# Gated DeltaNet chunk inverses: 32x32 diagonal blocks on VectorE and two doubling levels on TensorE, in place of 16x16 blocks and three levels

## The reference

```
A = where(strict, einsum('bhncd,bhnmd->bhncm', kb, k) * decay, 0)
T = triangular_solve(A + eye, eye, left_side=True, lower=True, unit_diagonal=True)
u = T @ vb
w = T @ (kb * exp(gc)[..., None])
# then per chunk: v_new = u_c - w_c @ S;  o_c = (q_c e^gc) @ S + attn_c @ v_new
#                 S = S e^g_last + (k_c e^(g_last-gc))^T v_new
```

## Time and profile before

| | us |
|---|---|
| Median of 3 runs | 2618.58 (2617.45 to 2620.59) |
| Profiled execution | 2620.2, span 2618.4 |
| TensorE busy | 2346.7 |
| VectorE busy | 1070.3 |
| ScalarE busy | 646.9 |

### The profile page before, as it was taken

How to read it: one execution, slowest core, us unless ns; L and a number is a source line. 1 busy time by engine, 2 the same in 40 slices (tenths; PEclk the granted TensorE clock), 3 DMA queues, 4 the chain that set the end, 5 groups by cost and what they waited for, 6 DMA issues and landing times. The chain is left out here.

```text
span 2618.4 us, 35138 instructions
## 1 busy us (share of the span) xinstructions
PE 2346.7 (90%) x13864; PEld 2160.8 (83%) x13864; DVE 1070.3 (41%) x1882; ACT 646.9 (25%) x1400; POOL 0.2 (0%) x4
## 2 busy tenths in 40 slices
PE   5888987569999999999997769796999999979898
PEld 3677876459999999999996559675999999968676
DVE  4132221345666665766664633353222222231233
ACT  4123222104233232243341100352111111131211
POOL 0000000000000000000000000000000000000000
PEclk6999988559999999999998579898999999989999
DMA  4010201411121121111201444442222222041432
GB/s 155 9 65 9 82 11 51 139 38 39 44 62 41 44 69 41 44 52 34 69 28 46 147 139 152 155 127 76 70 72 72 72 72 71 25 150 44 138 109 61
DMA packets 224158, 191.38 MB, mean 73 GB/s; under 512 B 30253, under 2 KB 197198, under 8 KB 224047
## 3 DMA queue, kind: packets, MB, share of 16 engines
q1 hardware_dynamic: 212792, 152.71, 20.1%
q10 hardware_dynamic: 11302, 37.82, 3.6%
HBM read 138.57 MB, written 52.11 MB: 73 GB/s over the span
## 5 line engine op out<-in xcount | busy, mean ns | idle before, releaser
L271 PE MATMUL bank<-xT_hi,w_lo 128*128 128x344 f32 x1152 | 391.5, 340 | 3.6 <-DVE w_lo L267 3.6
L273 PE MATMUL bank<-xT_hi,w_hi 128*128 128x344 f32 x1152 | 369.0, 320 | 0.0
L272 PE MATMUL bank<-xT_lo,w_hi 128*128 128x344 f32 x1152 | 368.8, 320 | 0.0
L271 PE MATMUL bank<-xT_hi,ffn_lo 128*128 128x344 f32 x1056 | 338.3, 320 | 12.3 <-DVE ffn_lo L267 12.3
L273 PE MATMUL bank<-xT_hi,ffn_hi 128*128 128x344 f32 x1056 | 337.8, 320 | 0.0
L272 PE MATMUL bank<-xT_lo,ffn_hi 128*128 128x344 f32 x1056 | 337.3, 319 | 0.0
L271 PEld LDWEIGHTS bank<-xT_hi,w_lo 128*128 128x128 f32 x1152 | 218.2, 189 | 3.7 <-issue 3.7
L272 PEld LDWEIGHTS bank<-xT_lo,w_hi 128*128 128x128 f32 x1152 | 218.3, 189 | 0.0
L273 PEld LDWEIGHTS bank<-xT_hi,w_hi 128*128 128x128 f32 x1152 | 217.4, 189 | 0.0
L271 PEld LDWEIGHTS bank<-xT_hi,ffn_lo 128*128 128x128 f32 x1056 | 199.3, 189 | 12.4 <-issue 12.4
L273 PEld LDWEIGHTS bank<-xT_hi,ffn_hi 128*128 128x128 f32 x1056 | 198.9, 188 | 0.0
(11 more groups left out here) (373 smaller groups left out, 4109.0 us busy)
## 6 DMA issues: line engine op xcount, KB each, us to landing
w_raw<-in_w_in SPq DMA_DIRECT2D x48, 512.0 KB, 3.9
ffn_raw<-in_w_ffn_in SPq DMA_DIRECT2D x44, 512.0 KB, 5.0
act_scr<-ffn_y ACTq DMA_DIRECT2D x22, 516.0 KB, 2.6
fo_sr<-act_scr SPq DMA_DIRECT2D x16, 704.0 KB, 6.6
fo_wr<-in_w_ffn_out SPq DMA_DIRECT2D x22, 512.0 KB, 5.2
gate_scr<-gate ACTq DMA_DIRECT2D x16, 516.0 KB, 2.9
a_kv_raw<-in_w_in SPq DMA_DIRECT2D x3, 2048.0 KB
mix_ta<-gate_scr SPq DMA_DIRECT2D x8, 516.0 KB, 4.9
```

Of the source, the lines that this page charges most:

```text
L271: nc.tensor.matmul(out, stat_lo, mov_hi, start=start, stop=False)
L272: nc.tensor.matmul(out, stat_hi, mov_lo, start=False, stop=False)
L273: return nc.tensor.matmul(out, stat_hi, mov_hi, start=False, stop=stop)
```

## The change

`SUB` goes from 16 to 32 and `LEVELS` from 3 to 2, so `base` is 32 partitions by 1024 elements in place of 64 by 256, and the level masks are those for blocks of 32 and 64. In `per_slot`, BASE gets 62 steps in place of 44, and TAIL 8 and 2 in place of 18 and 4; with one level of 6 less, a turn still has 144. `sqb`, a scratch tile of the key norms, now lies in `kbe`.

```diff
-LEVELS = 3
-SUB = 16
+LEVELS = 2
+SUB = 32
 NB = P // SUB
...
-            sqb = sb(s, "sqb", [P, 4, P])
+            sqb = kbe[:, :4]
...
-            per_slot = [10, 2, 3, 3, 44, 4] + LEVELS * [6] + [4, 2] + NT * [4] + [18, 4]
+            per_slot = [10, 2, 3, 3, 62, 4] + LEVELS * [6] + [4, 2] + NT * [4] + [8, 2]
...
-                    inc(nc.vector.tensor_tensor(sqb[:], kt4, kt4, ALU.mult), "sq")
+                    inc(nc.vector.tensor_tensor(sqb, kt4, kt4, ALU.mult), "sq")
...
-                    inc(nc.vector.reduce_sum(col[:, 0, 4 * b:4 * b + 4], sqb[:], AX.X), "ssq")
+                    inc(nc.vector.reduce_sum(col[:, 0, 4 * b:4 * b + 4], sqb, AX.X), "ssq")
...
-                       for s in (16, 32, 64)])
+                       for s in (32, 64)])
```

## The result

| us | before | after |
|---|---|---|
| Median of the runs taken together | 2619.59 (4 runs) | 2698.72 (2696.41 to 2700.8, 4 runs) |
| Ratio, 95% interval | | 1.0301 (1.0283 to 1.0319) |
| Span of the profiled execution | 2618.4 | 2696.1 |

What follows compares the result with a forecast made beforehand. TensorE, without a gap in seven of eight turns, was taken to bound the kernel. Seven turns at 13.2 + 0.3 + 1.7 − 5.4 = +9.8 us give +69, with the last head +76: 2695 us, range 2678 to 2718.

Steps and rivals of the forecast that it cites:

- the last head: Final head, only 48 steps and no bank wait: TensorE waits for late inverted blocks, +7 us.
- The inversion: On VectorE: 60 instructions with 9920 elements at 150 ns + 1.044 ns an element, 21.6 us, 15.2 us more.
- Rival 1: VectorE's inversion: flat price of small instructions, +8.4 us instead of +15.2, kernel at 2640 us; chance 6%.
- The stand at step 57: TensorE's projection step 57 waits for ScalarE's bank read, held by `gate` behind the inversion: 13.2 us a turn.
- The added steps cover nothing of it: The 18 steps added before the transpose (8.5 us) lie behind TensorE's wait; they cover only that for inverted blocks.
- The low clock: TensorE restarts at a granted clock of 0.50 after standing: 1.7 us a turn, 1.3 to 2.2.
- Margin at the first level: VectorE's backlog ends about 800, TensorE's first level product near 801: costed at nothing, up to 2 us a turn.
- Rival 2: At the first level, VectorE's backlog or a slow clock holds TensorE 2 to 4 us more a turn; chance 12%.
- The level: Dropping the middle doubling level saves TensorE 5.37 us a turn.
- The tail: End of a turn, TAIL cut to 8 and 2 steps: TensorE waits for `ob` multiplies, 0.3 us a turn.
- A turn: Each of seven head-loop turns: 13.2 + 0.3 + 1.7 − 5.4 = +9.8 us, to about 113 us.

Runs made afterwards that it cites:

- inversion_only: Kernel before with 32 chained minima of 275 elements added behind its inversion, levels and steps unchanged; 2745.21 us, ratio 1.0475.
- base_44: Kernel after with 44 instead of 62 steps in front of the transpose, the other 18 back in the tail; 2709.77 us, ratio 1.0348.
- gate_first: Kernel after with VectorE's step 25, the gate operation, moved in front of the inversion; 2659.62 us, ratio 1.015.
- order_only: Kernel after with all work kept and only VectorE's items reordered, among the inversion, first level and scan; 2630.22 us, ratio 1.0031.
- levels_only_even: Kernel before without the 16-to-32 level, its six steps given to the two remaining levels (9 each), tail unchanged; 2582.61 us, ratio 0.9853.
- quarter: order_only with each inversion block spread over four partitions, about a quarter of the elements, seven more loads and three more stores; 2626.08 us, ratio 1.0019.
- quarter_few: quarter with its DMAs joined: one load for the work rows, one for the four block copies, one store; 2686.78 us, ratio 1.0257.
- quarter_mix: quarter with only the load of the work rows joined, four issues in one; 2627.33 us, ratio 1.002.
- order66: order_only with four steps moved from the first slot to in front of the first level (66 instead of 62); 2640.0 us, ratio 1.0063.
- levels_only: Kernel before without the 16-to-32 level, inversion still 16x16, its six steps moved to the tail; 2596.34 us, ratio 0.9906.

## Why the prediction was right

The forecast was 2695 us, the result 2698.7, and the wait, its place and its cause are those that were named. That the sum is within 4 us is in part luck, since terms that were off have opposite signs: the stand is 0.5 us a turn shorter than forecast, the scan lost 0.65 us that nobody had named, and the last head cost 1.7 us less. Point by point:

- *The inversion*: forecast 21.6 us (15.2 more), measured 21.17 (768.65 to 789.82, 14.9 more than the 6.32 of before). The price per element held on shapes that the trace of before did not have. VectorE by line and shape:

```profile
L1948 DVE TENSOR_TENSOR base_prod<-base 32x240 f32<-32x240 f32 x16 | 6.3, 396 | 0.6
```

150 ns + 240 × 1.044 gives 401 ns; measured 396. Rival 1 (210 ns) falls. The prediction weighed this against the 58 cycles of the table in the Trainium skill ("VectorE: DVE Perf Modes", section on the TRN2 errata) and left out what that section says under its table: that the measured fixed term is nearer 150 cycles, and that a float32 tensor_tensor add of N elements takes (N + 151) cycles at 0.96 GHz. By that formula 240 elements would be 407 ns (an estimate); the trace has 396 for the multiply above and 398 for the add of the same size (L1951), within 3%. The table's row alone was the wrong thing to quote.
- *The stand at step 57*: forecast 13.2 us, measured 12.71, since the inversion grew by 14.9 and not 15.2 us and TensorE reached the step 21.80 us into its turn, which makes the slack 2.2 us and not 2.0. `inversion_only` and `base_44` showed that it is this step and not the transpose; `gate_first`, that it is the place of `gate` behind the inversion.
- *The added steps cover nothing of it*: shown by `base_44`, 12.7 us with or without them. That the transpose finds its blocks ready: forecast 9 us of margin (786 to 795), measured 11. But it was wrong to say that the added steps cover this wait. By the prediction's own numbers the transpose would come at 786.5 without them and find its blocks as well, and in `base_44` it does. They are needed for it only where the stand is gone, as in `order_only`.
- *The low clock*: forecast 1.7 us a turn (1.2 to 2.2), measured 13.18 − 72 × 0.1575 = 1.84. It is not the same in every turn: TensorE's busy time is 99.6 to 101.0 us in the seven, against 98.2 in the turns of `order_only` at a clock of 1.00, which is 1.4 to 2.8 us. The granted clock is 0.50 up to 797, 3.2 us behind the stand, and 1.00 from 798, in windows of 1 us:

```profile
796.00:797.00 1.00, 1.00 (x5) 1.00 (x5) 1.00 (x2) 0.00 (x0) 0.00 (x0) 0.50 0.00 0
797.00:798.00 1.00, 1.00 (x6) 1.00 (x5) 0.71 (x3) 0.00 (x0) 0.00 (x0) 0.63 0.23 24
798.00:799.00 1.00, 1.00 (x8) 1.00 (x7) 0.81 (x2) 0.00 (x0) 0.00 (x0) 1.00 0.93 264
```

- *Margin at the first level*: forecast level to within 1 us, measured 1.29 us: VectorE was waiting for TensorE there (L2221 above). Rival 2 did not come, and it was near.
- *The level*: forecast 5.37 us a turn. Alone (`levels_only_even`) a turn lost 4.5 us and had a wait of 0.6 of its own, so it is 5.1 to 5.4. The forecast of 24 matmuls fewer a turn was a slip: it is 48, as the 50 of the earlier trace rows besides the steps would have said; the time was read from the window and does not hang on it.
- *The tail*: forecast 0.3 us, measured 0.19 as idle time and 0.33 from start to start. Not foreseen: 0.45 us of idle time in the scan (832.30 above), 0.65 from start to start, where the work of VectorE that was pushed back stands in front of the first `vnew`.
- *A turn*: forecast +9.8 us; the turn shown took 113.34 against 103.03, +10.3. Seven turns took 794.4 us from the first store of `ea` to the last, against 721.2, so +73.2; everything behind the last of these stores, the last head among it, grew by 5.3 us (forecast 7), and what lies ahead shrank by 0.8. That is the 77.7 us between the spans, where 76 was forecast. TensorE's wait for `ub` in the last head rose from 3.1 to 15.6 us.
- *The range*: the bounds that the prediction lists come to −14 and +29 us, the range it states is −17 and +23. The result lies inside either.

The idle times and the clock come to 12.71 + 1.84 + 0.19 + 0.45 − 5.37 = 9.82 a turn, 0.5 us short of the turn shown. Counted from start to start on TensorE, where no modelled end of a matmul comes in, nothing is missing: from the turn's start to the transpose 47.69 us in place of 24.49, of which 18 steps are 8.51, so 14.70 for stand and clock; from there to the scan −8.26, or −5.43 without the level's six steps; scan +0.65, tail +0.33, what follows +0.06. That is 10.31. The step that would have been easy to miss was the first one: to look at which steps stand behind the inversion on VectorE, and not at the blocks that it makes. Where I was wrong was in the expectations: in `quarter`, `quarter_few`, `quarter_mix` and `order66` I took a shortening of one piece of the path for one of the path, and in `levels_only` and `base_44` I moved steps into the tail at no cost.

## What to carry to other kernels

Work moved from a full engine to one with idle time is free only if nothing stands in line behind it: list what the receiving engine does next, in its order, and who waits for that, before its share of busy time. Fill in front of the wait for a result covers that wait alone. And when one wait goes, read which comes last next: here it was the bank read (12.7 us), then a weight split (5.4), then the return of the blocks (3.3). Only with the first two gone and the third down to 1.0 was the change worth something, 12 us of the 39 that the level alone gives. Short waits can cost more than they last: turns with the same wait of 3.3 us differed by up to 3 us, by the granted clock behind it.

## What was not expected of the hardware

- Moving fill changed how often ScalarE loads its tables: five loads of 1.28 us a turn in `levels_only` and two in `levels_only_even`, which has the same operations. The Trainium skill ("ScalarE: Activation LUTs", section on what a table load costs) gives 1283 ns and some 1380 ns of drain for each switch. The loads agree to the nanosecond (1283 ns mean); the next operation started 0.02 us behind the load at 836.80, so this trace shows no drain behind it.
- One load of 512 KB that repeats its source four times (`quarter_few`) took 2.48 us to issue and was waited for 9.7 us from there, while four of 128 KB each took 0.60 us to issue and landed in about 2.5 us.
